# Last two experts' rows stacked on 128 partitions for one one-hot product, neither scattered; two chunks' sums on ScalarE, three chunks added by the store

## The reference, cut to what matters

```
cap = CAP_FACTOR * N // N_EXPERTS            # 64 sample rows, 16 prompt rows for each of 16 experts
g, idx = lax.top_k(jnp.swapaxes(aff, 1, 2), cap)
xs = jax.vmap(lambda hb, ib: hb[ib])(h, idx)
gu = jnp.einsum('becd,edf->becf', xs, w_gate_up)
y = jnp.einsum('becf,efd->becd', jax.nn.silu(gate) * up, w_down) * g[..., None]
ff = zeros((N, D)).at[idx].add(y)            # every expert adds its rows
x = layer_norm(ALPHA * x + gate2 * ff, ln2_g, ln2_b)
```

## Time and profile before

| what | value |
|---|---|
| median of 3 runs | 897.56 us (895.79 to 900.68) |
| the profiled execution: its own time | 900.26 us |
| its span, first to last instruction | 898.4 us |
| TensorE busy | 837.6 us, 93% |
| VectorE busy | 609.4 us, 68% |
| ScalarE busy | 220.2 us, 25% |
| GpSimd busy | 78.2 us, 9% |
| read from HBM, over the span | 259.03 MB |

### The profile page before, as it was taken

How to read it: one execution, slowest core, us unless ns; L and a number is a source line. 1 busy time by engine, 2 the same in 40 slices (tenths; PEclk the granted TensorE clock), 3 DMA queues, 4 the chain that set the end, 5 groups by cost and what they waited for, 6 DMA issues and landing times.

```text
span 898.4 us, 16492 instructions
## 1 busy us (share of the span) xinstructions
PE 837.6 (93%) x7183; PEld 424.1 (47%) x7183; DVE 609.4 (68%) x1026; ACT 220.2 (25%) x399; POOL 78.2 (9%) x110
## 2 busy tenths in 40 slices
PE   6889999799899987899999999999999999999985
PEld 5778978466678874233333333333232222222222
DVE  4669656789879887367755965685585585575267
ACT  2374456856832330000101010011001001001033
POOL 0010310001011011101101100110110110100000
PEclk9999999999999988999999999999999999999998
DMA  9931550450059289999999999999999999999955
GB/s 335 388 142 27 215 191 1 188 188 3 2 187 357 89 360 360 328 422 404 409 387 387 414 402 390 387 417 394 387 412 403 390 413 405 391 412 430 405 175 162
DMA packets 37347, 273.04 MB, mean 304 GB/s; under 512 B 5192, under 2 KB 5500, under 8 KB 24988
## 3 DMA queue, kind: packets, MB, share of 16 engines
q1 hardware_dynamic: 28832, 245.32, 68.0%
q0 software_dynamic: 7536, 24.00, 9.4%
q10 hardware_dynamic: 908, 2.68, 0.8%
HBM read 259.03 MB, written 14.00 MB: 304 GB/s over the span
## 4 chain that ended last, share of the span: by engine, by line
PE 62%; DMA 20%; DVE 10%; ACT 5%; issue 2%; SPq 0%; ACTq 0%; DVEq 0%
PE PS L1378 18%; DMA wr<-in_w_down 11%; PE PS L1381 9%; PE PS L1392 8%; DMA wr<-in_w_gate_up 7%; PE PS L982 4%; PE PS L984 4%; PE PS L983 4%; PE PS L1399 4%; PE PS L1197 2%; PE PS L1181 2%; PE PS L1220 1%; DMA ring<-in_w_mod 1%; PE PS L1151 1%; ACT xnT L670 1%
## 5 line engine op out<-in xcount | busy, mean ns | idle before, releaser
L1378 PE MATMUL PS<-wr,XT 128*32 128x512 f32 x2048 | 247.6, 600 | 7.6 <-DMA wr<-in_w_gate_up 5.3
L1378 PEld LDWEIGHTS PS<-wr,XT 128*32 128x32 f32 x2048 | 69.3, 111 | 161.9 <-issue 146.3
L1381 PE MATMUL PS<-wr,XT 128*32 128x512 f32 x1024 | 134.9, 596 | 0.0
L1392 PE MATMUL PS<-wr,HT 128*32 128x512 f32 x1024 | 122.1, 593 | 7.6 <-DMA wr<-in_w_down 7.6
L1913 DVE TENSOR_TENSOR h_s<-gate_s,PS 128x512 f32<-128x512 f32 x16 | 11.0, 688 | 164.9 <-ACT gate_s L914 164.9
L1904 DVE STREAM_TRANSPOSE XT<-Xg 32x256 f32<-32x256 f32 x180 | 115.4, 641 | 2.6
L914 ACT ACTIVATE gate_s<-PS 128x512 f32<-128x512 f32 x16 | 9.6, 597 | 323.0 <-PE PS L1381 323.0
L1928 DVE STREAM_TRANSPOSE HT<-h_s 32x256 f32<-32x256 f32 x128 | 82.1, 641 | 1.5
L1392 PEld LDWEIGHTS PS<-wr,HT 128*32 128x32 f32 x1024 | 33.6, 110 | 85.7 <-issue 66.2
L1381 PEld LDWEIGHTS PS<-wr,XT 128*32 128x32 f32 x1024 | 35.2, 111 | 76.3 <-issue 76.3
L1399 PE MATMUL PS<-wr,HT 128*32 128x512 f32 x512 | 67.0, 592 | 0.0
(11 more groups left out here) (316 smaller groups left out, 1106.4 us busy)
## 6 DMA issues: line engine op xcount, KB each, us to landing
wr<-in_w_gate_up SPq DMA_DIRECT2D x64, 2048.0 KB, 27.8
wr<-in_w_down SPq DMA_DIRECT2D x32, 2048.0 KB, 30.8
ring<-in_w_mod SPq DMA_DIRECT2D x24, 1024.0 KB, 10.3
ring<-in_w_in SPq DMA_DIRECT2D x4, 1024.0 KB, 9.9
ring<-in_w_out SPq DMA_DIRECT2D x4, 1024.0 KB, 6.2
w_qkv<-in_w_in SPq DMA_DIRECT2D x4, 768.0 KB, 13.5
h_scratch<-h POOLq DMA_DIRECT2D x5, 512.0 KB, 5.7
acc_scratch<-xt POOLq DMA_DIRECT2D x5, 512.0 KB, 6.4
```

The source lines that it names most:

```text
L1378: pe.matmul(PS[32 * j:32 * j + 32, 512 * b:512 * b + 512], x[:, 32 * (j % 2):32 * (j % 2) + 32], w[:, lo + 512 * (j // 2):lo + 512 * (j // ...
L1381: last = pe.matmul(PS[32 * j:32 * j + 32, 512 * GU_P_B:512 * GU_P_B + 512], x[:, CAP_S:SLQ], w[:, 512 * j:512 * j + 512], start=(k == 0), ...
L1392: pe.matmul(PS[32 * j:32 * j + 32, 512 * bs:512 * bs + 512], HT[e % 2][:, f, 32 * (j % 2):32 * (j % 2) + 32], w[:, lo + 512 * (j // 2):lo ...
```

## The change

1. The rows of expert 14 and expert 15 are put in one tile, `Y2`: expert 15's 64 sample rows on partitions 0 to 63, expert 14's on 64 to 127. One matrix `hot_s` of 128 partitions places both. The prompt rows of both go to `Yp` (partitions 64 to 79 and 96 to 111, the rest zero) with the matrix `hot_p`, and are multiplied once in full fp32, with no split.
2. Expert 14 is not scattered at all; no chunk is read late, and SP issues chunks 0 to 3 one after the other.
3. For expert 15 alone, the down product of the prompt rows is made of 256-wide pieces with all of the sum in one place, so that ScalarE's `odd_half` and VectorE's three instructions for it are replaced by four of 16x256.
4. ScalarE takes the sums of chunks 1 and 3 (before: 3). Chunks 0, 1 and 2 are stored by adding (before: 0 and 1), so a third piece of the output is written early with the bias.
5. TensorE starts with the identity products of chunks 0 and 1, then waits for the expert's rows. The banks change.

```diff
-FIN_BANK, FIN_ACT, FIN_ADD = (4, 2, 6, 0, 4), 3, 2
+FIN_BANK, FIN_ACT, FIN_ADD = (6, 4, 2, 0, 6), (1, 3), 3
-        sp.dma_start(iota[:], t["consts"][0:SL, P + 256:]).then_inc(misc_in, 16)
+        sp.dma_start(iota[:], t["consts"][:, P + 256:]).then_inc(misc_in, 16)
         for c in range(CH):
-            if c == 1:
-                sp.wait_ge(scattered, 16 * (NE - 1))
+        pool.memset(idx_last[:], -1.0)
-            if e == NE - 2:
-                pool.wait_ge(acc_in[0], 16)
-            if e:
+            if e == 1:
+                pool.wait_ge(mod_used, 6 * KC)
+                pool.memset(Yp[64:P, :], 0.0).then_inc(zeroed, 1)
+            if 0 < e < NE - 1:
                 scatter(e - 1)
@@ ScalarE
-        odd_half(NE - 1)
-        act.wait_ge(y_ok, NE + 2)
-        act.activation(yh[1][CAP_S:SL, :], ysc[1][CAP_S:SL, :], ACT.Copy).then_inc(yh_ok, 1)
+        def sums(c, i):
+            act.wait_ge(fin_ps, 2 * c + 2)
+            step(act.activation(xt[:, 3, :], PS[...], ACT.Copy, accum_out=fin[:, 0, i:i + 1]))
+            step(act.activation(nmr[:, c:c + 1], fin[:, 0, i:i + 1], ACT.Copy, scale=-1.0 / D))
+            step(act.activation(xt[:, 4, :], xt[:, 3, :], ACT.Square, bias=..., accum_out=fin[:, 1, i:i + 1]))
+            act.activation(fin[:, 0, i:i + 1], fin[:, 1, i:i + 1], ACT.Sqrt, ...).then_inc(std3_ok, 1)
         std3(0, 1)
+        sums(1, 0)
         scaled(0)
-        std3(1, 2)
+        std3(2, 2)
         scaled(1)
-        std3(2, 3)
+        sums(3, 1)
+        scaled(2)
+        std3(4, 3)
@@ TensorE
+                if e == NE - 1:
+                    for f in (2 * k, 2 * k + 1):
+                        for j in range(4):
+                            lo = 1024 * (f % 2) + 256 * j
+                            last = pe.matmul(PS[32 * j:32 * j + 32, 512 * bp:512 * bp + 256], HT[...][:, f, CAP_S:SLQ],
+                                             w[:, lo:lo + 256], start=(f == 0), stop=(f == KC - 1))
+                if c < PC:
+                    pe.wait_ge(yl_ok, 2 + h)
+                    pe.matmul(out, hot_s[:, c * P:(c + 1) * P], Y2h[:, cs], start=False, stop=False)
+                    pe.matmul(out, hot_s[:, c * P:(c + 1) * P], Y2l[:, cs], start=False, stop=True).then_inc(fin_ps, 1)
+                else:
+                    pe.matmul(out, hot_p[64:P, :], Yp[64:P, cs], start=False, stop=True).then_inc(fin_ps, 1)
+        out_rows(0)
+        out_rows(1)
+        pe.wait_ge(hot_ok, 2)
+        out_experts(0)
+        out_experts(1)
+        for c in range(2, CH):
+            out_rows(c)
+            out_experts(c)
@@ VectorE
+        for j in range(4):
+            cs = slice(D4 * j, D4 * j + D4)
+            last = dve.scalar_tensor_tensor(Yp[64:64 + CAP_P, cs], PS[32 * j:32 * j + CAP_P, 512 * bp:512 * bp + D4],
+                                            g_slot[CAP_S:SL, NE - 1:NE], G2[CAP_S:SL, cs], ALU.mult, ALU.mult)
+        last.then_inc(y_ok, 1)
+        fin_stats(0, 1)
+        centred(0)
+        inverse(0).then_inc(z_ok, 1)
+        centred(1)
+        fin_stats(2, 2)
+        inverse(1).then_inc(z_ok, 1)
         centred(2)
+        inverse(2).then_inc(z_ok, 1)
         centred(3)
-        fin_stats(4, 4)
+        fin_stats(4, 3)
         finished(3)
         centred(4)
         finished(4)
```

More of the change, by code:

```diff
@@ L193, in _build @@
     epsc = tile("epsc", [P, 1])
-    idx_last = tile("idx_last", [SL, 2])
+    idx_last = tile("idx_last", [P, 2])
     fin = tile("fin", [P, 2, 2])
@@ L266, in _build @@
     xf = [at(f"xf{c}", [P, D], Dz + 16384 * XF_SLOT + 4096 * c if c < PC else Dz + 16384 * XF_LAST) for c in range(CH)]
[L267 to L270, removed]
+    iota = at("iota", [P, NT], Fz)
+    hot_s, hot_p = at("hot_s", [P, N_S], Fz + 4096, F32R), at("hot_p", [P, P], Fz + 8192)
+    Y2, Yp = at("Y2", [P, D], Bz + 24576), at("Yp", [P, D], Bz + 28672)
+    Y2h, Y2l = at("Y2h", [P, D], Dz + 16384 * XF_LAST + 4096, F32R), at("Y2l", [P, D], Fz + 28672, F32R)
     ln2g = at("ln2g", [P, D], Fz + 32768)
@@ L1396, in _ @@
                     pe.wait_ge(hTp_ok, e + 1)
-                for j in range(4):
+                if e == NE - 1:
+                    for f in (2 * k, 2 * k + 1):
+                        for j in range(4):
+                            lo = 1024 * (f % 2) + 256 * j
+                            last = pe.matmul(PS[32 * j:32 * j + 32, 512 * bp:512 * bp + 256], HT[e % 2][:, f, CAP_S:SLQ],
+                                             w[:, lo:lo + 256], start=(f == 0), stop=(f == KC - 1))
+                for j in range(4 if e < NE - 1 else 0):
                     f, lo = 2 * k + j // 2, 1024 * (j // 2) + 512 * (j % 2)
@@ L1401, in _, with out_rows, out_experts @@
             last.then_inc(W_used, 1)
[L1403 to L1405 removed]
+        def out_rows(c):
             pe.wait_ge(acc_in[c], 16)
+            if c == 1:
+                pe.wait_ge(y_ok, NE - 1)
+            if c == 3:
+                pe.wait_ge(y_ok, NE + 2)
             if c == PC:
                 pe.wait_ge(z_ok, 1)
[L1409 to L1411 removed]
             for h in range(2):
[L1413 to L1421, removed]
+                pe.matmul(bank(FIN_BANK[c] + h), ident, xf[c][:, 512 * h:512 * h + 512], start=True, stop=False)
+        def out_experts(c):
             for h in range(2):
+                cs, out = slice(512 * h, 512 * h + 512), bank(FIN_BANK[c] + h)
                 if c < PC:
                     pe.wait_ge(yl_ok, 2 + h)
[L1425 to L1427 removed]
+                    pe.matmul(out, hot_s[:, c * P:(c + 1) * P], Y2h[:, cs], start=False, stop=False)
+                    pe.matmul(out, hot_s[:, c * P:(c + 1) * P], Y2l[:, cs], start=False, stop=True).then_inc(fin_ps, 1)
+                else:
+                    pe.matmul(out, hot_p[64:P, :], Yp[64:P, cs], start=False, stop=True).then_inc(fin_ps, 1)
+        pe.wait_ge(gu_ok, 2 * NE)
+        out_rows(0)
[6 more added lines that the diff above has]
+            out_experts(c)
     @block.vector
@@ L1893, in _ @@
         dve.tensor_copy(g_slot[CAP_S:SL, :], vp)
-        dve.tensor_tensor(idx_last[0:CAP_S, :], diff[:, NE - 2:NE], ib[:, NE - 2:NE], ALU.add)
-        dve.tensor_copy(idx_last[CAP_S:SL, :], ip[:, NE - 2:NE]).then_inc(slot_ok, 1)
+        dve.tensor_tensor(idx_last[0:64, 0:1], diff[:, NE - 1:NE], ib[:, NE - 1:NE], ALU.add)
+        dve.tensor_tensor(idx_last[64:P, 0:1], diff[:, NE - 2:NE - 1], ib[:, NE - 2:NE - 1], ALU.add)
+        dve.tensor_copy(idx_last[64:64 + CAP_P, 1:2], ip[:, NE - 1:NE])
+        dve.tensor_copy(idx_last[96:96 + CAP_P, 1:2], ip[:, NE - 2:NE - 1]).then_inc(slot_ok, 1)
         def x_turned(e):
@@ L1958, in y_evac, with y_lo @@
                 dve.wait_ge(g2_in, 32)
-            if e >= 2:
+            if 2 <= e < NE - 2:
                 dve.wait_ge(scattered, 16 * (e - 1))
[L1961 to L1967, removed]
+            if e == NE - 2:
+                dve.wait_ge(zeroed, 4)
+            y_sample_half(e, 0)
+            y_sample_half(e, 1)
+            y_prompt_rows(e).then_inc(y_ok, 1)
         def one_hot():
             dve.wait_ge(misc_in, 32)
[L1972 to L1979, removed]
+            dve.tensor_scalar(hot_s[:], iota[:, 0:N_S], idx_last[:, 0:1], None, ALU.is_equal).then_inc(hot_ok, 1)
+            dve.tensor_scalar(hot_p[64:P, :], iota[64:P, N_S:NT], idx_last[64:P, 1:2], None, ALU.is_equal).then_inc(hot_ok, 1)
+        def y_lo(n, rows, cs):
+            dve.wait_ge(yh_ok, n)
+            dve.tensor_tensor(Y2l[rows, cs], Y2[rows, cs], Y2h[rows, cs].bitcast(F32), ALU.subtract).then_inc(yl_ok, 1)
         dve.wait_ge(x_t, 2)
@@ L1993, in _ @@
         one_hot()
-        y_lo(0, 0, 0, D)
-        y_evac(NE - 1)
+        y_lo(1, slice(64, P), slice(0, D))
+        dve.wait_ge(W_used, DN_END[NE - 1] + 1)
+        for h in range(2):
+            y_sample_half(NE - 1, h).then_inc(y_ok, 1)
+        for h in range(2):
+            y_lo(2 + h, slice(0, 64), slice(H2 * h, H2 * h + H2))
+        bp = dn_banks(NE - 1)[1]
+        for j in range(4):
[3 more added lines that the diff above has]
+        last.then_inc(y_ok, 1)
         dve.wait_ge(ln2_in, 32)
@@ L2016, in inverse @@
             dve.wait_ge(std3_ok, c + 1)
-            return dve.reciprocal(rstd[:, c:c + 1], fin[:, 0, 0:1] if c == FIN_ACT else nmr[:, c:c + 1])
+            std = fin[:, 0, FIN_ACT.index(c):FIN_ACT.index(c) + 1] if c in FIN_ACT else nmr[:, c:c + 1]
+            return dve.reciprocal(rstd[:, c:c + 1], std)
         def finished(c):
```

36 lines of the change are left out of this document (12 added, 24 removed).

## The result

The changed kernel takes 900.72 us (median of 22 runs, 898.64 to 903.58), the kernel before 898.93 us (median of 22, 895.79 to 901.18). The ratio is 1.002, with an interval of 1.0011 to 1.0029: 0.2% slower, where 0.4% faster was forecast. The measured time also lies above the range (891.3 to 896.8).

The account below looks back on a forecast made before the run. Bound by the last down weights' load until 864.16 us, then mainly VectorE's list: -4.07 (VectorE) + 0.1 (TensorE) + 0.4 (stores) = -3.6 us, from 897.56 to 893.9 us, 0.4% faster; range 891.3 to 896.8.

Parts of the forecast that it names:

- The 1.35 us: End of the kernel: time from the prompt's store landing at 897.05 us to the span's end at 898.4.
- the third adding store ends last: Rival, final stores: taking 7 to 9 us, it lands at 893.5 to 895.5; time 894 to 896 us; chance 0.18.
- a store of 10.6 us: Adding store, slowest-load rival: it decides from 10.6 us on; at 17.0 us the time is 903 us; chance 0.02.
- the prediction's signs of being wrong: Profile after: ScalarE waits absent or above 3 us, clock 0.50, chunk 4's products behind 885.5, or an adding store landing last.
- VectorE's end: VectorE's norm list: ends at 890.34 us, 4.07 us earlier, before adding 0.1 us for TensorE's matmuls.
- Stretch of the stores: Final stores: the prompt's store, meeting the ends of two others, takes 3.0 us in place of 2.6, +0.4 us.
- The prompt rows: Expert 15's prompt rows on VectorE: four 16x256 instructions and no split, saving 3.13 us (bounds 2.1 to 3.6).
- the two waits for ScalarE: Norm: VectorE waits for ScalarE's means of chunks 1 and 3, 0.34 and 1.45 us, about 1.8 together.
- the arrival of `xf` with no wait: Chunk loads of `xf`: chunks 1 to 4 land near 868 to 872.6 us, before TensorE wants them; no gain counted.
- the clock at 1.00 to the last product: TensorE in the norm: full clock until near 884.7 us; the rival of a drop to 1.2 GHz had chance 0.06.
- The narrow matmuls: Expert 15's 256-wide matmuls on TensorE: 0.1 us for two units; the rival costing 1.8 us had chance 0.06.
- the rule on weight loads: Skill rule on TensorE: loads overlap matmuls only when the row group differs, so every added narrow-matmul load would show.

Follow-up runs that it names:

- e2: Kernel before, with GpSimd's last two waits (for its stores) moved to SP: ratio 0.9996 to the kernel before.
- e7: Changed kernel with no adding store, all five chunks scaled by VectorE and stored by SP, GpSimd's last waits on SP: ratio 0.9964 to before.
- e5: Changed kernel with two chunks stored by adding, GpSimd's last waits on SP, chunk 1's sums back on VectorE: ratio 0.9939 to before.
- e8: Repeat run of the changed kernel with two chunks stored by adding and GpSimd's last waits on SP: 894.11 us, ratio 0.9949 to before.
- e1: Changed kernel with GpSimd's last two waits (for its stores) moved to SP: 897.34 us, ratio 0.9983 to before.
- e6: Changed kernel, GpSimd's last waits on SP, GpSimd instead waiting at its end for VectorE's last result: one run, 897.75 us.
- e10: Kernel before, with chunk 2 also scaled by ScalarE and stored by adding, GpSimd's waits unmoved: 903.23 us, ratio 1.0043 to before.
- e3: Changed kernel with two chunks stored by adding, chunk 2 scaled by VectorE and stored by SP: 898.06 us, ratio 0.9987 to before.
- e4: Changed kernel with two chunks stored by adding and GpSimd's last waits on SP: 894.67 us, ratio 0.9947 to before.
- e9: Changed kernel with only chunk 0 stored by adding, GpSimd's last waits on SP: 894.38 us, ratio 0.9942 to before.

## Why the prediction was wrong

**The step that failed** is in the first part: "After it only the prompt's store is left: issued at 894.45, landed 2.6 us later, at 897.05, and 1.35 us more to the end of the span at 898.4." The 1.35 us were taken as a fixed piece behind the prompt's store. Some 0.5 us belong to the store (e2); the other 0.8 were the wait for GpSimd's DRAIN, which had run beside VectorE since 890.9. Two chains ended within a microsecond of each other, and only one had been followed. "A microsecond less on VectorE's list is therefore a microsecond less of time, if nothing else becomes later than it" stood on it, and GpSimd's last wait became later: 893.5 in place of 890.7.

**The rival that came nearest**, "the third adding store ends last", had the right engine and store and the wrong price. It took the landing as the end. With the DRAIN behind it, the break-even wasn't a store of 10.6 us but a landing at 898.4 - 7.7 = 890.7, the landing of before; and my own forecast had the third store land at 892.2. With the row of before that alone gives an end at 892.2 + 7.7 = 899.9, 1.5 us slower. None of the prediction's signs of being wrong would have caught it: no adding store landed last. The row stood in the trace of before, under the closing line of the program.

**The terms, counted from the last weights.** VectorE's end: forecast 4.07 - 0.1 earlier, measured 4.3. Prompt's store: forecast 3.0 us, measured 5.2, so 2.6 more than before in place of 0.4. From its landing to the end of the span: forecast 1.35, measured 6.4, so 5.0 more. -4.3 + 2.6 + 5.0 = +3.3, which is 37.5 - 34.2. The 2.6 has no price of its own in this sum: with a prompt's store of 2.6 us GpSimd's DRAIN would still have ended when it did, and the last term would be 7.6. The path that set the end is another: third adding store issued at 885.76 (forecast 886.5), landed 7.7 us later (forecast 5.7), and 7.8 us more to the end of the span (forecast: nothing). The medians differ by only 1.8 us; the profiled execution of the changed kernel was one of its slowest (903.32 in a range to 903.58), and single executions of one kernel scatter by some 5 us.

**Stretch of the stores.** The mechanism was right, the size was off by a factor of six. With no adding store each plain one takes 2.6 us (e7); with two chunks added the prompt's takes 2.6 to 3.1 (before, e2 to e5, e8), with three 3.7 to 5.2 (changed, e1, e6, e10). "DMA: Bandwidth & Descriptors" of the Trainium skill (Queues, rings and completion order) would have an engine take turns between the queues that have work; the longer times of both kinds where they meet agree with it, though no row shows the turns.

**What held.** The prompt rows (3.13 us forecast, 3.1 measured between the last weights and the first sums), the two waits for ScalarE (0.34 and 1.45 forecast, 0.35 and 1.20 measured), the arrival of `xf` with no wait, the clock at 1.00 to the last product, TensorE's last product (884.7 forecast, 883.6 measured), and nothing lost ahead of the last weights. One row was read too widely: at 875.36 only chunk 1 was there, and TensorE had stood for it alone; the trace has chunks 2 to 4 landing at 876.6 to 880.2. Nothing in the sum hangs on that. The narrow matmuls cost nothing, so the rule on weight loads in the Trainium skill, "TensorE: Matmul & The Clock Gate" (What overlaps and what doesn't), isn't borne out by 32-column weights on 128 rows.

**Shown, and only argued.** That GpSimd's DRAIN, by way of the third adding store, turned the change into a loss is shown by e1, e3 and e10. That the rest of the change is a gain is shown by e4, e5 and e9, which keep it (0.5 to 0.6% faster), beside e2, which has the moved waits without it (no change). How that gain divides between the stacked rows, the scatter left out, the 256-wide pieces and TensorE's order is not shown, since no run has one of them alone. The traces place it: e5's tail is 3.1 us shorter than e2's, VectorE's list of the norm is as long as before (16.65 against 16.7), and the 3.1 us lie ahead of it, between the last weights and the first sums. What the DRAIN does in its 7.3 us, and in the 3.6 us after a landing, stays open.

## What to carry to other kernels

Ask for the closing line of the program on every engine before taking the last visible transfer as the end: two chains can end together, and a wait blamed on an engine that has long been idle hides the real one. Where GpSimd issues DMAs, let its program end with the issue and put the waits for their completion on another engine; here that was worth 3.4 us (e3 to e4), for two waits moved, and nothing that the medians show where another chain ended as late (e2). Work moved to a slower path to spare the bounding engine pays only if that engine was not waiting anyway: here VectorE waited for ScalarE in the very place, so the third adding store saved it nothing.

## What the runs showed of the hardware

GpSimd's DRAIN at the end of a program took 7.2 to 7.4 us when its DMAs had landed before it began (before, changed, e3, e10) or landed early in it (e6). When it began at the issue of the last one (e1, e2, e4, e5, e7, e8, e9) it ended 3.4 to 3.7 us after the last landing and was up to 19.4 us long (e7). SP's took 7 ns; ScalarE's and VectorE's lasted as long as the engine's last instruction (0.3 and 1.3 us), TensorE's until its last product had ended (5.0 to 6.3 us).

The section The DRAIN you can't avoid of "VectorE: DVE Perf Modes" in the Trainium skill gives the DRAINs of a program's preamble and postamble as about 12 ns, constant, on all five engines. Whether the DRAINs of L131, a line of the kernel, are of that kind no row shows: SP's is near that figure, and GpSimd's is six hundred times it.

An adding store of 512 KB took 5.2 to 8.5 us, a plain one 2.6 us alone and up to 7.6 us beside adding ones (e4).
